# Half of the feed-forward input weights' low halves from a negation on ScalarE and an adding transfer

## What is computed

```
D_MODEL = 1024; SEQ = 512; D_FF = 2816; DEPTH = 2

def swiglu_ffn(h, w_in, w_out):
    gate, up = jnp.split(h @ w_in, 2, axis=-1)
    return (jax.nn.silu(gate) * up) @ w_out

for i in range(DEPTH):
    x = x + 0.5 * swiglu_ffn(rmsnorm(x, ffn1_norm[i]), ffn1_w_in[i], ffn1_w_out[i])
    ...                       # mixer i and memory attention, then their output product
    x = x + 0.5 * swiglu_ffn(rmsnorm(x, ffn2_norm[i]), ffn2_w_in[i], ffn2_w_out[i])
return rmsnorm(x, final_norm)
```

## Time and profile before

| | before |
|---|---|
| runs (us) | 2438.24, 2434.68, 2438.74; median 2438.24 |
| span of the profiled execution, first to last instruction (us) | 2435.8 (its own device time isn't listed apart from the runs; they lie 1.1 us under to 2.9 us over the span) |
| busy: TensorE / its weight loads / VectorE / ScalarE / GpSimd (us) | 2406.4 / 1958.1 / 1212.4 / 748.4 / 302.1 |
| memory read / written (MB) | 226.55 / 10.49 |
| loads of `ffn_w_in` | 176 of 512 KB, median 3.8 us from issue to landing |
| granted clock of TensorE, mean | 0.997 of full speed |

### The profile page before, as it was taken

How to read it: one execution, slowest core, us unless ns; L and a number is a source line. 1 busy time by engine, 2 the same in 40 slices (tenths; PEclk the granted TensorE clock), 3 DMA queues, 4 the chain that set the end, 5 groups by cost and what they waited for, 6 DMA issues and landing times.

```text
span 2435.8 us, 30558 instructions
## 1 busy us (share of the span) xinstructions
PE 2406.4 (99%) x11046; PEld 1958.1 (80%) x11046; DVE 1212.4 (50%) x1447; ACT 748.4 (31%) x1014; POOL 302.1 (12%) x284
## 2 busy tenths in 40 slices
PE   8999999999999999999999999999999999999998
PEld 7978888877888788888878888877788887888876
DVE  6554443355888654444444444344347634444422
ACT  4432222234444322222223222223333222222222
POOL 3500000111333310000110000220001111000021
PEclk9999999999999999999999999999999999999999
DMA  7833332332222333333333333332223233333332
GB/s 218 255 108 94 95 95 88 94 112 61 78 69 77 96 95 93 92 93 94 95 94 93 92 92 94 95 106 84 70 86 87 78 95 95 95 94 91 91 93 79
DMA packets 438942, 237.92 MB, mean 98 GB/s; under 512 B 8180, under 2 KB 434272, under 8 KB 438880
## 3 DMA queue, kind: packets, MB, share of 16 engines
q1 hardware_dynamic: 434160, 223.37, 31.4%
q0 software_dynamic: 4704, 13.69, 1.6%
q10 hardware_dynamic: 16, 0.00, 0.0%
HBM read 226.55 MB, written 10.49 MB: 97 GB/s over the span
## 4 chain that ended last, share of the span: by engine, by line
PE 96%; DVE 2%; issue 1%; ACT 1%; DMA 0%; POOL 0%; ACTq 0%; DVEq 0%; POOLq 0%; SPq 0%
PE acc L824 30%; PE acc L826 30%; PE acc L825 30%; PE mix L240 1%; PE mix L227 1%; PE mix L662 1%; PE mix L375 0%; DVE tmp L1059 0%; ACT w_hi L1281 0%; DVE x L1212 0%; PE mix L369 0%; PE mix L362 0%; PE mix L350 0%; PE mix L589 0%; DVE w_lo L993 0%
## 5 line engine op out<-in xcount | busy, mean ns | idle before, releaser
L993 DVE TENSOR_TENSOR w_lo<-raw,w_hi 128x1024 fp32r<-128x1024 f32 (+1 forms) x424 | 546.4, 1291 | 639.7 <-ACT w_hi L1281 628.1
L824 PE MATMUL acc<-h_hi,w_hi 128*128 128x512 f32 x2048 | 820.4, 401 | 3.9 <-DVE h_lo L1063 3.9
L826 PE MATMUL acc<-h_hi,w_lo 128*128 128x512 f32 x2048 | 808.5, 395 | 0.0
L825 PE MATMUL acc<-h_lo,w_hi 128*128 128x512 f32 x2048 | 808.3, 395 | 0.0
L1281 ACT ACTIVATE w_hi<-raw 128x1024 fp32r<-128x1024 f32 (+1 forms) x424 | 437.3, 1035 | 352.6 <-DMA raw<-in_ffn_w_out_dram 263.4
L824 PE MATMUL acc<-act_hi,w_hi 128*128 128x512 f32 (+1 forms) x1280 | 482.9, 377 | 5.2 <-DVE act_lo L1003 4.3
L826 PE MATMUL acc<-act_hi,w_lo 128*128 128x512 f32 (+1 forms) x1280 | 478.1, 374 | 0.0
L825 PE MATMUL acc<-act_lo,w_hi 128*128 128x512 f32 (+1 forms) x1280 | 478.1, 374 | 0.0
L824 PEld LDWEIGHTS acc<-h_hi,w_hi 128*128 128x128 f32 x2048 | 385.4, 188 | 96.7 <-DVE h_lo L1063 5.2
L825 PEld LDWEIGHTS acc<-h_lo,w_hi 128*128 128x128 f32 x2048 | 385.5, 188 | 91.4 <-issue 3.4
L826 PEld LDWEIGHTS acc<-h_hi,w_lo 128*128 128x128 f32 x2048 | 385.2, 188 | 91.5
(11 more groups left out here) (191 smaller groups left out, 1167.0 us busy)
## 6 DMA issues: line engine op xcount, KB each, us to landing
raw<-in_ffn_w_in_dram SPq DMA_DIRECT2D x176, 512.0 KB, 3.8
raw<-in_ffn_w_out_dram SPq DMA_DIRECT2D x64, 512.0 KB, 4.0
raw<-in_hgrn_w_in_dram SPq DMA_DIRECT2D x40, 512.0 KB, 3.9
raw<-in_gmlp_w_in_dram SPq DMA_DIRECT2D x40, 512.0 KB, 3.8
raw<-in_mem_w_kv_dram SPq DMA_DIRECT2D x32, 512.0 KB, 4.5
raw<-in_ffn_w_out_dram SPq DMA_DIRECT2D x32, 384.0 KB, 3.3
raw<-in_gmlp_w_out_dram SPq DMA_DIRECT2D x24, 512.0 KB, 3.9
raw<-in_hgrn_w_out_dram SPq DMA_DIRECT2D x16, 512.0 KB, 4.0
```

What stands on the lines that cost most here:

```text
L824: pe.matmul(bank, w_hi[:, j, i, :], hi, start=(start and i == 0), stop=False)
L825: pe.matmul(bank, w_hi[:, j, i, :], lo, start=False, stop=False)
L826: m = pe.matmul(bank, w_lo[:, j, i, :], hi, start=False, stop=(stop and i == last))
L993: dve.tensor_tensor(w_lo[:, j, 0:nkb], raw[:, j, 0:nkb], f32(w_hi[:, j, 0:nkb]), ALU.subtract).then_inc(w_lo_ready, 1)
```

## The change

In an "ffn_in" phase the low halves of lanes 2 and 3 are made in another way. ScalarE, right behind the rounding, writes the negative of `w_hi` into `w_lo` (`less_hi`, by the activation Copy with scale -1). GpSimd waits for that (`w_less_hi`) and issues a transfer that reads the weights from memory a second time and adds them to what stands in `w_lo`. TensorE waits for that transfer (`w_rest_summed2`, `w_rest_summed3`, one semaphore per lane, since two may be under way). VectorE does no subtraction for these lanes and raises `w_lo_ready` by 2 at the place of the first, so that its count stays right. Lanes 0 and 1, and all other phases, are as before.

```
@@ -814,9 +814,11 @@
-            def unit(q, j, operands, bank, start, stop, each=None):
+            def unit(q, j, operands, bank, start, stop, each=None, summed=None):
 
                 pe.wait_ge(w_lo_ready, LANES * q + j + 1)
+                if summed is not None:
+                    pe.wait_ge(sem(f"w_rest_summed{j}"), 16 * summed)
...
@@ -884,7 +886,7 @@
                 if kind == "ffn_in":
                     def body(it, first=False):
                         for j in range(LANES):
-                            in_unit(ph, s, it, j, first)
+                            in_unit(ph, s, it, j, first, (FB // 2) * n_ffn + it + 1 if j >= 2 else None)
...
@@ -1125,11 +1127,10 @@
-                        lo(ph.q0 + it, 2)
+                        dve.sem_inc(w_lo_ready, 2)
                         if first:
                             norm_stats(s)
                         gate(0)
-                        lo(ph.q0 + it, 3)
                         up(1)
...
@@ -1343,11 +1344,16 @@
+                        def less_hi(j):
+                            act.wait_ge(w_hi_ready, LANES * (ph.q0 + it) + j + 1)
+                            act.activation(w_lo[:, j], f32(w_hi[:, j]), ACT.Copy, scale=-1.0).then_inc(sem("w_less_hi"), 1)
                         hi(ph.q0 + it, 2)
+                        less_hi(2)
                         if first:
                             root(s)
                         silu(0)
                         hi(ph.q0 + it, 3)
+                        less_hi(3)
...
@@ -1540,9 +1546,19 @@
-            s = 0
+            s = n_ffn = 0
             for i, (kind, ph) in enumerate(phases):
-                if kind == "hgrn_in":
+                if kind == "ffn_in":
+                    w = ffn_w[n_ffn][0]
+
+                    for it in range(FB // 2):
+                        for j in (2, 3):
+                            at = ((j % 2) * FB + 2 * it + j // 2) * P
+                            pool.wait_ge(sem("w_less_hi"), FB * n_ffn + 2 * it + j - 1)
+                            pool.dma_start(w_lo[:, j], w[:, :, at:at + P],
+                                           accum_op=ALU.add).then_inc(sem(f"w_rest_summed{j}"), 16)
+                    n_ffn += 1
```

More of the change, by code:

```diff
@@ L867, in _, with in_unit @@
             h_parts = [(h_hi[:, k, :], h_lo[:, k, :]) for k in range(DB)]
-            def in_unit(ph, s, it, j, first=False):
+            def in_unit(ph, s, it, j, first=False, summed=None):
                 def each(i):
@@ L873, in in_unit @@
                 pe.wait_ge(acc_read, ph.g0 + LANES * it + j - 3)
-                unit(ph.q0 + it, j, h_parts, acc[j][:], True, True, each if first and j == 0 else None)
+                unit(ph.q0 + it, j, h_parts, acc[j][:], True, True, each if first and j == 0 else None, summed)
                 if first and j == 0:
@@ L1541, in _ @@
             store_v(7, 3)
-            s = 0
+            s = n_ffn = 0
             for i, (kind, ph) in enumerate(phases):
-                if kind == "hgrn_in":
+                if kind == "ffn_in":
[7 more added lines that the diff above has]
+                    n_ffn += 1
+                elif kind == "hgrn_in":
                     att, hg = mixes[i]
```

## The result

| | before | after |
|---|---|---|
| median of the runs (us) | 2437.02 (4 runs) | 2557.91 (2553.67 to 2564.2, 4 runs) |
| ratio, 95% interval | | 1.0497 (1.0483 to 1.0511) |
| span of the profiled execution (us) | 2435.8 | 2559.9 |
| TensorE busy / not busy in the span (us) | 2406.4 / 29.4 | 2437.1 / 122.8 |

Slower by 121 us, three times the 40 us that were forecast, and inside the range.

A forecast was written before the change was run, and what follows sets the result against it. TensorE was taken as the bound, so only its waiting counts. 40 steady quads at 1.0 us add 40 us to the 2435.8 us span: 2475.8, or 2478 us as the runs' median (+1.6%); range 2434 to 2630.

The forecast's parts named there:

- TensorE is the bound, and relief of VectorE pays nothing: Feed-forward input: removing 88 VectorE subtractions, 108 us, gains 0, since only whether TensorE is made to wait counts.
- ScalarE's negation at no cost: 88 added ScalarE activations of 1.045 us each fit into its idle time of 3.1 or 4.9 us; cost 0.
- Time allowed for lane 2, 6.4 us: Steady quads: from GpSimd's issue at about 263.6 to TensorE's first weight load of unit 2 at 270.02.
- Issue to landing: Lane 2's adding transfer: first bytes 1.5, A 3.6, shared weight load 1.8, landing 0.4; 7.3 us, 0.9 over what is allowed.
- A: DMA engines' work for one adding transfer, two reads and the write: bounded by 1.8 and 5.5 us, taken as 3.6.
- two loads: Choice for the adding transfer's engine work: twice one 512 KB weight load's 1.8 us, so 3.6 us.
- sharing with a weight load: Lane 0's next weight load falls into the same stretch as lane 2's transfer and shares the engines: 1.8 us.
- 0.1 for the restart: TensorE's restart after each steady quad's pause: 0.1 us on top of 0.9 late, 1.0 us per quad.
- First quad of a phase: neither stalls: In 4 of 44 quads lane 2 is allowed some 11 us and lane 3 7.7 us, so no stall.
- the dear add: Rival: three moves one after another, A 5.5 us, 4.6 us per steady quad, 1.5 per first quad; 2628 us; chance 30%.
- Lane 3 hidden in steady quads: Lane 3's transfer lands at 276.3, before unit 3 would start anyway at 276.6; no further stall.
- Hidden: Rival: accumulation at a plain transfer's rate, A 1.8 us, lands in 5.5 us, below 6.4; no change, 2438 us; chance 27%.

## Why the prediction was right in direction and wrong in size

Three steps failed: the landing time of lane 2 was under-sized, the first quad of a phase was read wrongly, and the clock had no term.

*TensorE is the bound, and relief of VectorE pays nothing:* right; the kernel without the transfer is at 0.9996. ScalarE's negation at no cost: right, likewise.

*Time allowed for lane 2, 6.4 us:* nearly right, 6.2. GpSimd woke 0.3 us after the negation's end, not at once.

*Issue to landing, "1.5 + 3.6 + 1.8 + 0.4 = 7.3 us":* under-sized; it is 7.9 to 8.9 for lane 2 in steady quads, median 8.4 (the 7.8 of the page is over both lanes). The 1.5 us before the first bytes held the 0.94 us of writing of a plain transfer; with the add it is 1.55, 0.6 more. A is 4.2, not 3.6: the chosen "two loads" were priced at the hardware queue's 1.8 us, while a plain software transfer of this shape here takes 2.8 of the engines., which seemed to price both queues alike, says little of this shape: the software queue's 4704 packets there average 2.9 KB, not 512 B. The add's factor itself is 1.5 (4.2 over 2.8). "The bandwidth ceiling" in the Trainium skill's "Collectives: The Full Stack" gives, for the ring of a collective, a rate halved by the two source reads; these runs show less than that against the plain software transfer. The 1.8 us for sharing with a weight load was right: 2 us. An estimate with the measured terms is 1.5 + 0.6 + 4.2 + 1.8 + 0.4 = 8.5. The steady pauses are 1.95 us on average, in place of the 0.9 forecast: 42 us more over 40 quads.

*"0.1 for the restart":* also too small. The quad from the restart at 261.37 to that at 285.70 is 24.33 us at full clock: 22.40, the pause of 1.66, and 0.27. That is 7 us more.

*No term for the clock:* this step was missing. After 10 of the 40 steady pauses, and in three of the four first quads, TensorE was granted half its clock for some 3 us, 1.5 us lost each time: 16 us in the steady quads, some 5 in the first ones. The quads show it: 24.3 us where the clock stayed (261.37 to 285.70), 26.2 where it fell (1080.56 to 1106.76). With 0.27 us for each of 45 pauses these 20 us are about the 30.7 us by which TensorE's busy time grew; it returned to 2406.7 when the pauses were gone.

*"First quad of a phase: neither stalls":* wrong. I took the matmul at 1268.08 in the earlier trace rows for the start of unit 0; it is the eighth and last piece of it. Unit 0's first seven pieces had run before, and only the last waited for the last `h_lo`. The trace before says so: a matmul on `h_hi` stands before the gap, and VectorE takes the quad's unit 3 here (TensorE and VectorE, kernel before):

```profile
1266.02 0.40 PE L826 MATMUL acc<-h_hi,w_lo 128*128 128x512 f32 x1
...
1286.66 0.69 DVE L1115 TENSOR_TENSOR tmp<-acc,rstd 128x512 f32<-128x512 f32 x1
```

Unit 3 ended by 1286.6, so it began by 1281.0, not at 1285.9: at most 2.8 us were allowed, not 7.7, for a landing of 6.4. In the first quads of the four phases the changed kernel pauses 3.9, 3.4, 2.1 and 3.7 us for lane 3, in the third 1.5 us for lane 2 as well, and in the other three it pays the half clock on top. Between VectorE's takings of unit 0 and unit 3 it needs 4.1 to 5.8 us more in each, 21 us in all.

*The sum again:* 21 us in the four first quads, the rest of 124 over 40 steady ones: 2.6 us each, 1.95 of pause, 0.27 of restart and 0.4 of half clock. I had 1.0. Against the 84 us that were missing stand thus about 42 of landing, 7 of restart, 16 of half clock and 21 of first quads, 86 together. That 2558 us still lies in the stated range is the width left for the dear add, not this sum.

*Lane 3 hidden in steady quads:* right, in the changed kernel none of the pauses there is lane 3's; alone, it has four there, 4.3 us in all.

*The rivals:* the dear add had the right term, but its three moves (5.5 us) were too many. Hidden was refuted as built, yet it holds once the issues are moved 3.8 and 2.9 us forward.

Open: why the clock falls behind some pauses and not behind others of nearly the same length. It fell behind steady pauses of 1.8 to 2.5 us and stayed at 1.00 behind one of 2.8 us (ended at 212.93). No run was made for it. Nor does a run show why lane 2's transfer lands sooner when it is issued from its earlier place.

## What to carry to other kernels

Before work is moved from an idle engine to a transfer, compare the transfer's whole way (writing of descriptors, both readings, one concurrent load, landing) with the time from its last input to its use; here 2 us of lateness decided, paid in every turn of the loop. If TensorE is the bound, a pause can cost more than its length: here 93 us of pauses cost 124. If such a transfer must be, move its inputs forward in the issuing engine's order: that was free here, while keeping other transfers out of its way only made a new wait.

## What the hardware showed beyond that

An adding transfer of 1024 pieces of 512 B occupies GpSimd for 1.55 us to write, a plain one of the same shape 0.88; it uses 4.2 us of the 16 engines against 2.8. With a weight load beside it, lane 2's lands in 7.9 to 8.9 us, without one in 6.4. Pauses of about 2 us in a stream of matmuls were followed by some 3 us of half clock in 10 of 40 cases, 1.5 us lost in each. DMA traffic at a share of 0.70 left the pitch of TensorE's matmuls where it was (1004 in 234 us).
